# A hybrid encoder step: the recurrence's steps placed among the input projections, and the first unit's terms placed among the first transposes

## The chip, the cores and the metric

The kernel runs on one core of a Trainium2 chip. The metric is the device time of one execution in microseconds; all times below are microseconds from the first instruction of the profiled execution unless a unit is given.

## The reference

Two layers of an encoder run over 544 frames of 1024 features: 512 frames of a new stream and 32 frames of a running one, whose state is given. Only the mixer of layer 0 is touched.

```python
z = rmsnorm(x) @ w_in                    # (544, 3584): qa, ka, va | fb, ib, qb, gb, 512 each
qa, ka = rmsnorm per head of 64 with q_gain, k_gain
f = lb + (1 - lb) * sigmoid(fb);  logf = log(f);  kb = 1 - f;  qb = silu(qb);  vb = ib
# mixer A: softmax attention of 8 heads with a relative-position bias over (qa, ka, va)
# mixer B: S_t = diag(f_t) S_{t-1} + k_t v_t^T,  o_t = S_t^T q_t, in blocks
ob = rmsnorm per head(o) * out_gain * silu(gb)
x = x + concat(oa, ob) @ w_out
# then a mixture of 32 experts (2 for each frame); layer 1: short convolution, then experts
```

All inputs are float32. The outputs are the frames, the new keys and values, and the recurrence's and the convolution's new states.

## The kernel before

Every engine has an instruction list of its own, written out by hand; semaphores order them. Frames stand in five blocks `c` of 128, 128, 128, 128 and 32 (`ROWS`).

**Projections.** The 3584 columns of `w_in` are 14 groups of 256 (`HG`), in the order `GROUPS`: ib (groups 0, 1), fb (2, 3), qb (4, 5), gb (6, 7), qa (8, 9), ka (10, 11), va (12, 13). SyncE loads a group into one of three slots `wab` once the group three before it is done (`z_mm`, L355). ScalarE writes the rounded high part `wab_hi` (`group_hi`, L1075), GpSimd the rest `wab_lo` by one subtraction (L565). TensorE runs a group as units: five (one per block of frames) or, for groups 2 to 7, four (feature tile by half of the frames, transposed output). A unit is 24 matmuls: for each of 8 slices of the features, high by high, high by low and low by high (L661, L662). Unit `u` writes bank `u % 4` and waits until the unit four before it has been read out (`z_free`). There are 64 units, 0 to 63. Unit 0 alone runs its 8 terms with `wab_lo` last.

**The start.** Per block: ScalarE squares a block of frames (`square`), VectorE scales it to `XN` (`norm`, L1297), TensorE transposes it (`norm_transpose`, L637), ScalarE writes the high part `xc_hi`, VectorE the low part `xp_lo` (`mixer_in_lo`). TensorE transposes blocks 0 and 1, then unit 0, the transposes of block 2, unit 1, and so on.

**Read-out.** ScalarE turns groups 2 to 7 into `fT`, `qdecT`, `gateT`. Behind group 3, VectorE and ScalarE make `kinT` (keys with inverse decay) and `dec` from logarithm, scan and exponentials. For qa and ka, ScalarE squares a unit, VectorE sums (L1394, L1395), ScalarE takes the root, VectorE scales from the bank (L1398, which frees it) and multiplies by the gain.

**Recurrence.** For each block: transposes of `kinT` (`hgrn_keys`, L705) to `kr`; products of keys and queries (`hgrn_products`, L715), masked to `am`; state updates in groups of 32 frames (`hgrn_updates`, L731), chained by VectorE into states `st` (`hgrn_chain`, L1453, L1455); outputs (`hgrn_out`, L751 from `am`, L756 from `st`); ScalarE squares them, VectorE sums and scales them to `ot` (`hgrn_norm`, L1430); transposes of `ot` (`hgrn_T`, L767); VectorE multiplies by `gateT` into `zB` (`hgrn_gate`). Keys and products stand among the units of groups 12 and 13, together with the transposes of q and k (`rows_T`); updates, outputs and what follows stand behind the last unit, before the attention.

**Attention.** Scores (L806), VectorE adds the bias and takes the maximum (L1489), ScalarE the exponential (L1158), TensorE transposes (L823) and multiplies by the values (L839). `bias` is loaded from copies in device memory that SyncE writes early (L353) and reads behind the last unit (L367). Then follow the output projection (L880) and the experts, whose weights arrive in a stream.

## Time and profile before

| | |
|---|---|
| runs shown | 1215.63, 1217.22, 1218.97; median 1217.22 |
| profiled execution | 1213.17 |
| its span, first to last instruction | 1211.4 |
| TensorE matmul busy | 1019.1 (84%) |
| VectorE, ScalarE, GpSimd busy | 426.4, 289.8, 181.0 |
| mean granted TensorE clock | 0.92 |

The span is what the trace covers; the execution's own time is 1.8 longer. The granted clock is the share of full speed that the chip gave TensorE; its two levels are 1.2 GHz (0.50) and 2.4 GHz (1.00). A busy share is a mean over stages that have different limits, so it does not say what a stage waits for.

### The profile page before, as it was taken

To read this page: it belongs to the slowest core of one execution; us is meant where nothing else is said; L and a number is where in the kernel's file an instruction comes from. 1 tells how busy PE (TensorE), PEld (TensorE's weight loads), DVE (VectorE), ACT (ScalarE), POOL (GpSimd) and SP (SyncE) were. 2 spreads that over 40 slices of the span, in tenths; PEclk is the share of its full clock that TensorE was granted. 3 is DMA by queue.
4 is the path that set the end of the run, shared out by engine and by line. 5 is a ranking of instruction groups with operands and counts; after the bars stand their busy time and mean duration, and the time that the engine had idled before them with its cause. 6 is when DMAs were issued, how large, how long until landed. Compare 5 with 4: busy or idle time off the path is not lost.

```text
span 1211.4 us, 20104 instructions
## 1 busy us (share of the span) xinstructions
PE 1019.1 (84%) x8635; PEld 797.5 (66%) x8635; DVE 426.4 (35%) x907; ACT 289.8 (24%) x551; POOL 181.0 (15%) x146
## 2 busy tenths in 40 slices
PE   4998999777999899878778289999998999778771
PEld 4988999644689765444444089999997554444440
DVE  5324475356733611111101474555436111011104
ACT  4144332114721312111101332122212211111110
POOL 4334332002000023222111000000000122221110
PEclk9999999855989999999889689999999999888896
DMA  6322221411074599999997923324566999999966
GB/s 216 83 79 70 81 98 48 96 28 53 1 262 165 232 362 417 416 416 416 416 416 302 279 45 101 105 60 150 209 106 265 364 417 416 417 416 417 414 254 231
DMA packets 114862, 282.83 MB, mean 233 GB/s; under 512 B 22954, under 2 KB 70102, under 8 KB 98356
## 3 DMA queue, kind: packets, MB, share of 16 engines
q1 hardware_dynamic: 105044, 263.66, 58.5%
q0 software_dynamic: 9728, 17.85, 4.0%
q8 instruction: 70, 1.15, 0.4%
q14 instruction: 20, 0.16, 0.0%
HBM read 270.57 MB, written 27.02 MB: 246 GB/s over the span
## 4 chain that ended last, share of the span: by engine, by line
PE 59%; DMA 24%; DVE 7%; SPq 4%; ACT 2%; issue 2%; POOL 1%; DVEq 0%; POOLq 0%; ACTq 0%
DMA w<-in_w_dram 19%; PE banks L1015 12%; PE banks L943 12%; PE banks L880 9%; PE banks L662 8%; PE banks L954 4%; PE banks L661 3%; SPq L389 3%; DMA wab<-in_w_in_ab_dram 2%; DMA yab<-y_rows 1%; PE banks L637 1%; POOL wab_lo L565 1%; PE banks L839 1%; PE banks L823 1%; PE banks L937 1%
## 5 line engine op out<-in xcount | busy, mean ns | idle before, releaser
L943 PE MATMUL banks<-w,xgT 128*64 128x256 f32 x2048 | 253.2, 406 | 74.9 <-DMA w<-in_w_dram 73.7
L943 PEld LDWEIGHTS banks<-w,xgT 128*64 128x64 f32 x2048 | 159.4, 147 | 177.3 <-DMA w<-in_w_dram 77.4
L1662 DVE TENSOR_TENSOR hh<-banks,sg 128x128 f32<-128x128 f32 x64 | 18.7, 292 | 409.1 <-ACT sg L1230 409.1
L577 POOL DMA_INDIRECT y_rows<-ys,yidx x64 | 63.7, 995 | 383.3 <-ACT ys L1238 381.9
L954 PE MATMUL banks<-w,hT 128*64 128x512 f32 x512 | 116.9, 598 | 0.0
L1015 PE MATMUL banks<-xc_hi,wc_hi 128*128 128x272 f32 x384 | 111.4, 290 | 2.1 <-DVE xc_lo L1309 2.1
L1015 PE MATMUL banks<-xc_hi,wc_lo 128*128 128x272 f32 x384 | 111.7, 291 | 0.0
L1015 PE MATMUL banks<-xc_lo,wc_hi 128*128 128x272 f32 x384 | 110.9, 289 | 0.0
L573 POOL DMA_INDIRECT xr<-x_rows,gidx x32 | 33.5, 1046 | 412.4 <-DVE yidx L1648 394.4
L662 PE MATMUL banks<-wab_hi,xc_hi 128*128 128x256 f32 (+1 forms) x320 | 91.1, 285 | 0.7 <-POOL wab_lo L565 0.7
L662 PE MATMUL banks<-wab_hi,xp_lo 128*128 128x256 f32 (+1 forms) x320 | 90.1, 282 | 0.0
L662 PE MATMUL banks<-wab_lo,xc_hi 128*128 128x256 f32 (+1 forms) x320 | 88.4, 280 | 0.0
L1230 ACT ACTIVATE sg<-banks 128x128 f32<-128x128 f32 x64 | 17.8, 278 | 295.1 <-PE banks L943 295.1
L565 POOL TENSOR_TENSOR wab_lo<-wab,wab_hi 128x2048 fp32r<-128x2048 f32 x14 | 67.3, 4816 | 121.7 <-ACT wab_hi L1075 121.7
L1015 PEld LDWEIGHTS banks<-xc_hi,wc_hi 128*128 128x128 f32 x384 | 72.9, 190 | 2.7 <-issue 2.5
L1015 PEld LDWEIGHTS banks<-xc_lo,wc_hi 128*128 128x128 f32 x384 | 72.9, 190 | 0.0
L1015 PEld LDWEIGHTS banks<-xc_hi,wc_lo 128*128 128x128 f32 x384 | 72.7, 189 | 0.0
L954 PEld LDWEIGHTS banks<-w,hT 128*64 128x64 f32 x512 | 34.0, 136 | 58.7 <-issue 54.8
L661 PE MATMUL banks<-xc_hi,wab_hi 128*128 128x272 f32 x192 | 57.0, 297 | 6.7 <-POOL wab_lo L565 6.7
L1238 ACT ACTIVATE ys<-banks 128x512 f32<-128x512 f32 x64 | 38.2, 597 | 97.9 <-PE banks L954 97.9
L661 PE MATMUL banks<-xc_hi,wab_lo 128*128 128x272 f32 x192 | 56.9, 296 | 0.0
L662 PEld LDWEIGHTS banks<-wab_hi,xc_hi 128*128 128x128 f32 (+1 forms) x320 | 55.6, 174 | 1.7 <-POOL wab_lo L565 1.0
(283 smaller groups left out, 1796.0 us busy)
## 6 DMA issues: line engine op xcount, KB each, us to landing
w<-in_w_dram SPq DMA_DIRECT2D x192, 1024.0 KB, 23.2
wab<-in_w_in_ab_dram SPq DMA_DIRECT2D x13, 1024.0 KB, 5.0
wc<-in_w_in_c_dram SPq DMA_DIRECT2D x24, 512.0 KB, 5.7
yab<-y_rows SPq DMA_DIRECT2D x16, 512.0 KB, 6.8
wo<-in_w_out_ab_dram SPq DMA_DIRECT2D x4, 1024.0 KB, 5.6
x_rows<-XF SPq DMA_DIRECT2D x8, 512.0 KB, 2.6
wo<-in_w_out_c_dram SPq DMA_DIRECT2D x4, 1024.0 KB, 5.7
H<-in_x_prompt_dram SPq DMA_DIRECT2D x4, 512.0 KB, 8.4
```

Source lines behind the costliest of these rows:

```text
L389: sp.dma_start(w13[s][:, part, :, :], w[l, bass.ds(e, 1)].rearrange("e (p k) f -> p (e k) f", p=P)).then_inc(done, 16)
L565: pool.tensor_tensor(wab_lo[n % 3][:], wab[n % 3][:], wab_hi[n % 3][:].bitcast(F32), ALU.subtract).then_inc(w_lo, 1)
L573: pool.indirect_dma_start(xr[i][:, :], None, x_dram[l][:, :], bass.IndirectOffsetOnAxis(ap=index.bitcast(U32), axis=0), bounds_check=T - 1 ...
L577: pool.indirect_dma_start(y_dram[l][:, :], bass.IndirectOffsetOnAxis(ap=index.bitcast(U32), axis=0), ys[i][:, :], None, bounds_check=4 * T ...
L661: return pe.matmul(out, w[:, k, cols], x[:, k, t], **flags)
L662: return pe.matmul(out, x[:, k, t], w[:, k, :], **flags)
L880: last = pe.matmul(bank[i % 4][0:ROWS[c], 0:OW], z(a, k)[:, c * P:c * P + ROWS[c]], w(b, k, s), start=k == 0 and j == 0, stop=k == KT - 1 ...
L943: last = pe.matmul(bank[hb][64 * f:64 * f + 64, 0:2 * P].rearrange("p (w j) -> p w j", w=2), xgT[i][:, k, 64 * ab:64 * ab + 64], w13[s][:, ...
L954: last = pe.matmul(bank[6 + ab][64 * n:64 * n + 64, :], hT[ab][:, 64 * f:64 * f + 64], w2s[s][:, f, n * 512:(n + 1) * 512], start=f == 0, ...
L1015: last = pe.matmul(bank[3 * half + a][:, 0:HALF], w[s][:, k, a, :], x[:, k, half * HALF:(half + 1) * HALF], start=k == 0 and j == 0, stop= ...
L1238: act.activation(ys[e % 4][:], bank[6 + ab][:, :], ACT.Copy).then_inc(ys_ok, 1)
L1662: dve.tensor_tensor(hh[ab][:], bank[3 + ab][:, P:2 * P], sg[ab][:], ALU.mult).then_inc(hh_ok, 1)
```

## The change

1. **Start.** The two halves of the first weights are waited for and rounded one by one, with `xc_hi` of block 0 between them. Unit 0's terms with `wab_hi` run behind the transposes of block 0, then the transposes of blocks 1 and 2, then its terms with `wab_lo`. ScalarE's rounding of group 1 moves ahead of the square of block 4.
2. **Weights.** Group 3's load is issued ahead of the bias copies. ScalarE rounds group `n + 3` before the logarithm and the exponentials. GpSimd's subtraction is four instructions.
3. **Recurrence.** Keys and products stand behind units 27 to 31, the first updates behind unit 32, outputs behind units 34, 37, 40, 43 and 46 with the transposes of the block before and the updates of the next, the last transposes behind unit 48. Units 26 to 48 use banks 0 and 1 only; banks 2 to 7 belong to the recurrence. Unit 49 waits for all states and all of `zB`. The memory of `st`, `am`, `kr`, `osq`, `zB`, `bias` and one output weight moves.
4. **q and k.** ScalarE squares each head with a sum of its own, copies the unit to `q_tok` or `k_tok` and thereby frees the bank; VectorE scales in place. The gain of q moves into the copy behind its transposes.
5. **SyncE.** The state is loaded behind group 9, the new states are stored behind group 13's load, `bias` is loaded behind unit 53, and the first output weight no longer waits for `zB`.

```diff
+SHARED = range(FIRST[6], FIRST[11])
+UNIT_BANK = [u % 2 if u in SHARED else u % 4 for u in range(UNIT_END[-1])]
...
 @block.sync
-            sp.wait_ge(rev_ok, 1)
-            sp.dma_start(revs_dram[:, :, 0:639], bc(rev[:, 0:639].unsqueeze(1), [NH, 32, 639])).then_inc(rb_dma, 16)
             for n in range(3, 14):
                 sp.wait_ge(z_mm, UNIT_END[n - 3])
                 group_load(n)
+                if n == 3:
+                    sp.wait_ge(rev_ok, 1)
+                    sp.dma_start(revs_dram[:, :, 0:639], bc(rev[:, 0:639].unsqueeze(1), [NH, 32, 639])).then_inc(rb_dma, 16)
+                if n == 9:
+                    sp.wait_ge(hg_ok, 2)
+                    sp.dma_start(st[NPR][:], state_hgrn[0, 0].rearrange("(a b) k v -> (b k) a v", b=2)).then_inc(st_in, 16)
+            sp.wait_ge(st_ok, 4)
+            sp.dma_start(nh_p[0, 0].rearrange("(a b) k v -> (b k) a v", b=2), st[NPR - 1][:]).then_inc(sh_out, 16)
...
-            sp.wait_ge(z_mm, UNIT_END[-1])
+            sp.wait_ge(z_mm, UNIT_END[11])
...
-            sp.wait_ge(zB_ok, NC)
 @block.gpsimd
-                pool.tensor_tensor(wab_lo[n % 3][:], wab[n % 3][:], wab_hi[n % 3][:].bitcast(F32), ALU.subtract).then_inc(w_lo, 1)
+                for k in range(0, KT, 2):
+                    last = pool.tensor_tensor(wab_lo[n % 3][:, k:k + 2, :], wab[n % 3][:, k:k + 2, :],
+                                              wab_hi[n % 3][:, k:k + 2, :].bitcast(F32), ALU.subtract)
+                last.then_inc(w_lo, 1)
 @block.tensor
                 if u_ >= 4:
-                    pe.wait_ge(z_free[u_ % 4], u_ // 4)
+                    pe.wait_ge(z_free[b], freed(u_, b) - 1)
+                if u_ == SHARED.stop:
+                    pe.wait_ge(st_ok, NC)
+                    pe.wait_ge(zB_ok, NC)
...
                 if u_ == 0:
+                    norm_transpose(0, 1)
+                    norm_transpose(0, 2)
                     pe.wait_ge(w_lo, 1)
...
             for n in range(1, 14):
                 pe.wait_ge(w_lo, n + 1)
                 for a in range(UNITS[n]):
                     unit(n, a)
+                    beside = FIRST[n] + a - SHARED.start
+                    if 1 <= beside <= NC:
+                        hgrn_keys(beside - 1)
+                        hgrn_products(beside - 1)
+                    if beside == 6:
+                        hgrn_updates(0)
+                    if 8 <= beside <= 20 and beside % 3 == 2:
+                        c = (beside - 8) // 3
+                        if c > 0:
+                            hgrn_T(c - 1)
+                        hgrn_out(c)
+                        if c + 1 < NC:
+                            hgrn_updates(c + 1)
+                    if beside == 22:
+                        hgrn_T(NC - 1)
                     if n >= 12:
                         rows_T(NC * (n - 12) + a)
-                        i = NC * (n - 12) + a
-                        (hgrn_products if i % 2 else hgrn_keys)(i // 2)
-            hgrn_updates(0)
-            for c in range(NC):
-                if c + 1 < NC:
-                    hgrn_updates(c + 1)
-                if c > 0:
-                    hgrn_T(c - 1)
-                hgrn_out(c)
 @block.scalar
             square(0, 0)
-            group_hi(0)
-            for c in range(1, NC):
+            first_hi(0)
+            mixer_in_hi(0, [0])
+            first_hi(1).then_inc(w_hi, 1)
+            square(0, 1)
+            for c in range(2, NC):
                 square(0, c)
                 mixer_in_hi(0, [c - 1])
+                if c == 3:
+                    group_hi(1)
...
+                for h in range(heads):
+                    last = act.activation(qsq[i % 2][0:n, h * HD:(h + 1) * HD], bank[b][0:n, h * HD:(h + 1) * HD], ACT.Square,
+                                          accum_out=hss[0:n, sl + h:sl + h + 1])
+                last.then_inc(qsq_ok, 1)
+                act.activation((q_tok if i < 2 * NC else k_tok)[0:n, c, lo:lo + HG], bank[b][0:n, 0:HG], ACT.Copy).then_inc(z_free[b], 1)
+                act.wait_ge(qsq_ok, i + 1)
+                act.activation(hms[0:n, sl:sl + heads], hss[0:n, sl:sl + heads], ACT.Sqrt, bias=epsc[0:n, 0:1], scale=1.0 / HD).then_inc(qrt_ok, 1)
+                if i // 3 < NC and i % 3 == 0:
+                    hgrn_square(i // 3)
+                if i // 3 < NC and i % 3 == 1:
+                    hgrn_root(i // 3)
 @block.vector
             for i in range(4 * NC):
...
+                if i % 3 == 0 and 0 < i // 3 < NC:
+                    hgrn_gate(i // 3 - 1)
+                dve.wait_ge(qrt_ok, i + 1)
+                dve.reciprocal(hrs[0:n, sl], hms[0:n, sl]).then_inc(qms_ok, 1)
+                dve.wait_ge(qms_ok, i + 1)
+                scaled = dve.tensor_tensor(d, d, bc(hrs[0:n, sl].unsqueeze(2), four), ALU.mult)
...
+                c, step = divmod(i, 3)
+                if c < NC and step == 0:
+                    if c + 1 < NC:
+                        hgrn_chain(c + 1, 0)
+                    hgrn_sums(c)
+                    if c + 1 < NC:
+                        hgrn_chain(c + 1, 1)
+                if c < NC and step == 1:
+                    hgrn_norm(c)
+                if c == NC - 1 and step == 2:
+                    hgrn_gate(c)
```

## Rows read from the trace of the kernel before

**Rows 1.** The chain that ended last, to 200: start, us, what

```profile
13.12 4.08 DVE XN L1297
...
37.45 5.71 PE banks L662 x46
...
43.16 17.04 DMA wab<-in_w_in_ab_dram
...
62.21 4.55 POOL wab_lo L565
...
66.81 13.87 PE banks L661 x96
...
103.90 5.00 POOL wab_lo L565
...
108.94 25.92 PE banks L661 x192
...
134.86 59.48 PE banks L662 x504
```

**Rows 2.** The timeline: first updates on TensorE, first softmax instruction on VectorE

```profile
230.23 0.91 PE L731 MATMUL banks<-vb,kr 32*64 32x64 f32 x64
...
279.18 0.29 DVE L1489 CUSTOM_DVE_ANT_0 sneg<-banks,bias 128x128 f32<-128x128 f32 x1
```

**Rows 3.** Stretches: us, busy time of PE, PEld, DVE, ACT, POOL, clock, DMA share, GB/s

```profile
220.00:230.00 10.00, 10.00 (x151) 9.31 (x151) 1.91 (x5) 1.73 (x4) 0.00 (x0) 1.00 0.01 2
...
240.00:250.00 10.00, 5.17 (x155) 3.74 (x154) 4.03 (x9) 0.90 (x2) 0.00 (x0) 0.50 0.40 132
...
290.00:300.00 10.00, 7.94 (x32) 3.75 (x32) 6.67 (x14) 3.63 (x13) 3.82 (x1) 0.50 0.00 0
```

**Rows 4.** The timeline, TensorE in unit 0

```profile
19.43 0.41 PE L662 MATMUL banks<-wab_hi,xc_hi 128*128 128x256 f32 x1
...
19.65 0.41 PE L662 MATMUL banks<-wab_hi,xp_lo 128*128 128x256 f32 x1
```

**Rows 5.** Groups by line, VectorE's XN: busy us, mean ns, idle before

```profile
L1297 DVE SCALAR_TENSOR_TENSOR XN<-H,rstd,gmix 128x1024 f32<-128x1024 f32 x5 | 9.2, 1842 | 0.8 <-DMA gmix<-in_norm_mix_dram 0.6
```

**Rows 6.** The timeline, TensorE in the recurrence's steps

```profile
202.51 0.60 PE L705 MATMUL banks<-ident,kinT 128*128 128x128 f32 x4
...
252.49 1.28 PE L731 MATMUL banks<-vb,kr 32*64 32x64 f32 x64
...
256.38 0.67 PE L751 MATMUL banks<-vb,am 32*32 32x64 f32 x16
...
256.98 0.47 PE L756 MATMUL banks<-st,qdecT 64*32 64x64 f32 x16
...
257.38 0.67 PE L751 MATMUL banks<-vb,am 32*32 32x64 f32 x16
```

**Rows 7.** The timeline, ScalarE: exponential with sum, read of the sum, next exponential

```profile
279.51 0.40 ACT L1158 ACTIVATE pr<-sneg,nmaxs 128x128 f32<-128x128 f32 x1 [0.70 <-DVE nmaxs L1489]
...
279.82 0.19 ACT L1158 ACTIVATION_READ_ACCUMULATOR pr<-sneg,nmaxs 128x1 f32 x1
...
279.91 0.39 ACT L1158 ACTIVATE pr<-sneg,nmaxs 128x128 f32<-128x128 f32 x1
```

**Rows 8.** Groups by line on ScalarE and VectorE: value copies, ot, chain steps

```profile
L1137 ACT ACTIVATE va<-banks 128x256 f32<-128x256 f32 (+1 forms) x10 | 3.8, 379 | 26.0 <-PE banks L662 26.0
...
L1430 DVE TENSOR_TENSOR ot<-banks,hrs 128x512 f32<-128x512 f32 (+1 forms) x5 | 3.4, 689 | 0.2
...
L1455 DVE TENSOR_TENSOR st<-tmpS,dec 128x256 f32<-128x256 f32 x16 | 6.8, 425 | 0.5
```

**Rows 9.** The timeline: VectorE beside GpSimd's subtractions

```profile
181.51 3.96 DVE L1395 TENSOR_SCALAR hms<-hss 128x4 f32<-128x4 f32 x1
...
290.48 4.42 DVE L1511 TENSOR_TENSOR dg<-ident,rinv 128x1024 f32<-128x1024 f32 x1
...
287.25 6.57 POOL L560 TENSOR_TENSOR wo_lo<-wo,wo_hi 128x2048 fp32r<-128x2048 f32 x1
```

More of the change, by code:

```diff
@@ L306, in freed @@
         def freed(unit, b):
-            return len([u for u in range(unit + 1) if u % 4 == b])
+            return len([u for u in range(unit + 1) if UNIT_BANK[u] == b])
         class Chain:
@@ L693, in rows_T @@
                     pe.wait_ge(qkT_ok, i - 1)
+                else:
+                    pe.wait_ge(zt_ok, NC)
                 for m in range(4):
@@ L701, in hgrn_keys @@
                     pe.wait_ge(hg_ok, 2)
-                else:
-                    pe.wait_ge(a_ok, c)
+                if c >= 2:
+                    pe.wait_ge(ko_ok, c - 1)
                 for m in range(4):
-                    last = pe.transpose(bank[4][0:ROWS[c], m * P:(m + 1) * P], kinT[:, m, c * P:c * P + ROWS[c]], ident[:])
+                    last = pe.transpose(bank[6 + c % 2][0:ROWS[c], m * P:(m + 1) * P], kinT[:, m, c * P:c * P + ROWS[c]], ident[:])
                 last.then_inc(ko_mm, 1)
             def hgrn_products(c):
-                pe.wait_ge(ko_ok, c + 1)
+                if c < 2:
+                    for b in range(2 + 2 * c, 4 + 2 * c):
+                        pe.wait_ge(z_free[b % 4], freed(SHARED.start - 1, b % 4))
+                else:
+                    pe.wait_ge(a_ok, c - 1)
                 for m in range(4):
@@ L714, in hgrn_products @@
                             head = slice(64 * par, 64 * par + 64)
-                            last = pe.matmul(bank[4 + par][PAIR * r:PAIR * r + PAIR, m * PAIR:(m + 1) * PAIR], kinT[head, m, t],
+                            last = pe.matmul(bank[2 + 2 * (c % 2) + par][PAIR * r:PAIR * r + PAIR, m * PAIR:(m + 1) * PAIR], kinT[head, m, t],
                                              qdecT[head, m, t], start=True, stop=True)
@@ L730, in hgrn_updates @@
                             cols = slice((2 * m + par) * HD, (2 * m + par + 1) * HD)
-                            last = pe.matmul(bank[r][64 * par:64 * par + 64, m * HD:(m + 1) * HD], kr[c][rows, cols],
+                            last = pe.matmul(bank[2 + r][64 * par:64 * par + 64, m * HD:(m + 1) * HD], kr[c][rows, cols],
                                              vb[rows, c, cols], start=True, stop=True, tile_position=(PAIR * r, 64 * par))
@@ L799, in scores @@
                     pe.wait_ge(s_ok, 2 * j)
+                else:
+                    pe.wait_ge(qkT_ok, 2 * NC)
+                    for b in range(4):
+                        pe.wait_ge(z_free[b], freed(UNIT_END[-1] - 1, b))
                 if c == 4:
@@ L1112, in _ @@
                     act.wait_ge(z_mm, un + 1)
-                    act.activation(dst[:, m, half * HALF:(half + 1) * HALF], bank[un % 4][:, 0:HALF], fn).then_inc(z_free[un % 4], 1)
+                    act.activation(dst[:, m, half * HALF:(half + 1) * HALF], bank[UNIT_BANK[un]][:, 0:HALF], fn).then_inc(z_free[UNIT_BANK[un]], 1)
+                    if 1 <= un - SHARED.start <= NC:
+                        hgrn_key_rows(un - SHARED.start - 1)
             for i in range(4 * NC):
@@ L1437, in hgrn_gate, with hgrn_chain @@
                 dve.wait_ge(zt_mm, c + 1)
-                dve.tensor_tensor(zB[:, :, t], bank[4 + c % 2].rearrange("p (m t) -> p m t", m=4)[:, :, 0:n],
+                dve.tensor_tensor(zB[:, :, t], bank[2].rearrange("p (m t) -> p m t", m=4)[:, :, 0:n],
                                   gateT[:, :, t], ALU.mult).then_inc(zB_ok, 1)
-            def hgrn_chain(c):
+            def hgrn_chain(c, half):
+                groups = range(ROWS[c] // PAIR)[2 * half:2 * half + 2]
                 dve.wait_ge(u_mm, c + 1)
-                if c == 4:
+                if c == 4 and half == 0:
@@ new lines, in rows_T @@
+            def rows_T(i):
+                kind, c = divmod(i, NC)
+                src = bank[6 + i % 2][:, :].rearrange("p (m t) -> p m t", m=4)[:, :, 0:ROWS[c]]
+                dst = kT[:, :, c * P:c * P + ROWS[c]] if kind else qT[:, c, :, 0:ROWS[c]]
+                dve.wait_ge(qkT_mm, i + 1)
+                if kind:
+                    dve.tensor_copy(dst, src).then_inc(qkT_ok, 1)
+                else:
+                    dve.tensor_scalar(dst, src, qgain[:, 0:1], None, ALU.mult).then_inc(qkT_ok, 1)
```

238 lines of the change are left out of this document (113 added, 125 removed).

## Prediction

> **What bounds the kernel now.** I read the slices of the page first: TensorE is busy nearly everywhere until 420 us, then the expert weights' transfers set the pace. The change touches only the first layer's mixer, so the question is what that stretch loses today. The chain of waits, in order of time, answers it for the projections [rows 1]: TensorE is the chain except where it waits for a split of the weights. Three such places stand out. Group 3 starts at 66.81, groups 4 to 6 have two smaller waits, and the first frames wait for VectorE's `XN`. The timeline then shows the largest loss: the recurrence's first updates are issued at 230.23, when the projections are done, and VectorE's first softmax instruction of the attention comes at 279.18 [rows 2]. The stretches [rows 3] show what these 49 us are: TensorE half idle and its granted clock at 0.50 (1.2 GHz), after 1.00 (2.4 GHz) at 220 us where it was busy without a gap. The clock is still 0.50 at 290 to 300, inside the attention.
>
> **Units of price.** 504 matmuls of 256 columns take 59.48 [rows 1], so 0.118 each and 2.83 a unit (24 matmuls); at 272 columns I scale to 0.1254, 3.01 a unit, 12.04 a group of four. At 1.2 GHz the same matmuls start 0.22 apart [rows 4], 5.2 a unit.
>
> **The start, and first unit's terms among the transposes.** `XN` of frame block 1 took 4.08, where five took 9.2 in all, so 1.3 for each other one [rows 1, 5]. GpSimd's subtraction of the first weights, one instruction, ran beside it; it now comes in four. VectorE can wait for a piece, a quarter of 4.6, so 1.3 to 2.5: saved 1.6 to 2.8. The 16 terms of unit 0 that need no `wab_lo` come ahead of the transposes of blocks 1 and 2 and leave the path behind `XN`: 1.9 at 2.4 GHz, 3.5 at 1.2, I take 2.6. Against it: ScalarE now rounds both halves of the weights and copies `xc_hi` before the square of block 1, about 1 later, and the transposes of block 2 wait for that block's `XN`, which also comes one step later. I take 3.0 (0 to 4.4). Group 1 then no longer waits for `wab_lo`, since its rounding moves ahead of the last square; that is 0.8 more, estimated from the start at 37.45. **+3.8**.
>
> **Other orders of the weights.** Groups 1 and 2 are 14.2 and 12.0 of matmuls behind 37.45, so TensorE is ready at 63.65 and waits until 66.81: 3.2. The cause is group 3's load, which landed 17.04 after its issue behind the bias copies in the same queue [rows 1]. It now goes first, and the copies, needed late, have the time. Group 3 takes 13.87 instead of 12.04, because the clock must come back: 1.8. From its end, 80.68, two groups need 24.1, but group 6 starts at 108.94: waits of 4.2, for splits that ScalarE starts only behind its exponentials. They now come ahead of these. Groups 6 and 7 take 25.92 instead of 24.1: 1.8. The hidden cost is that the recurrence's inputs (logarithm, sums, exponentials) start a rounding later, 1.9, but their group ends 7 us earlier; they are due two units into group 6. **+11.0**. The load of the HGRN state and both state stores move ahead of the bias loads on SP. Their waits are met before SP's next load is due, or only outputs are queued behind them. The first output weights lose the wait for `zB`; they arrive about as late behind the start of the attention as now. These at nothing; if SP were held, a weight load needs 5 us and has a whole group (14) as cover.
>
> **The 49 us.** The steps leave the end of the projections: 48.95 from 230.23 to 279.18 go, and 1.5 remain for the last transposes, their copy and the fill of `bias` (estimated from the sizes). **+47.5**.
>
> **What TensorE does in their place.** Transposes and products of the keys only move, at equal cost. Into groups 7 to 10 come [rows 6]: updates, 0.91 at 2.4 GHz against 1.28 at 1.2, four and a short one: 4.0. The transposes of `ot`, like those of `kinT` 0.60, four and a short one: 2.8. The outputs: one quarter of a block starts 1.00 behind the last one at 1.2 GHz, so 4.0 a block; full clock was never seen. Lower bound half of it, upper bound no less than 4.0. Updates gained a factor 0.71, and I take that: 2.8, and 2.6 for the short block, which has the same four hand-overs: 13.8 in all (9.9 to 19.7). Switches between kinds of matmul: 1.5. **-22.1**.
>
> **Do the steps hide?** In this stage projections have two banks, so ScalarE must free a bank within one unit, 2.83. Squares with sums at 128 columns start 0.40 apart, the read of the accumulator included [rows 7]. For 64 columns I take 0.35 (bounds 0.2, the read alone, and 0.40), four make 1.4; the copy is 0.38 [rows 8]; the bank is free 1.8 behind the unit and with the root (0.2, estimated) the work is 2.0 (at most 2.3). It fits. Rounding a group's weights (1.9) fills a gap once in five units and delays one bank by some tenths.
>
> The round of three units is 8.5 + 0.6 + 2.8 + 0.9 = 12.8. On VectorE: updates ready at 4.3, eight chain steps of 0.425 with 0.03 between (3.7), the sums as long as `ot` (0.7): 8.7. The next unit ends at 7.1, ScalarE is done at 9.1, root and `ot` at 10.3 [rows 8]. So 2.5 to spare before the next round needs `ot`.
>
> **One new wait.** Unit 49 waits for all of `zB`. The last gate stands on VectorE behind key unit 14, which waits for ScalarE: 2.0, then 1.4 for three small instructions and the gate, less 0.4 of transposes: TensorE is idle 3.0, with all of groups 11 to 13 and the attention queued behind it. A wait of 3.2 cost 1.8 in clock, so 1.8 here too. **-4.8**.
>
> **The attention's start.** At 290 to 300 TensorE was busy 7.94 at 0.50 [rows 3]; at full clock that is 4 less in ten, 8 in twenty at best. VectorE and ScalarE take over part of the pace. VectorE's `dg` took 4.42, 3.3 of it until GpSimd's subtraction of the output weights was through [rows 9]; this can recur. I take **+5** (0 to 8).
>
> **A rule against the change.** VectorE's 181.51 instruction of four columns took 3.96, and `dg` ended 1.1 behind GpSimd's [rows 9]. The Trainium skill (SBUF — State Buffer, Who interferes with whom) says that VectorE and GpSimd share a port pair which one holds for a whole instruction, and that a VectorE instruction with both inputs in SBUF contends with a GpSimd instruction that reads SBUF. By that rule, the trace agrees. The new scaling reads `q_tok` and sums from SBUF, where it read a bank; the reduce and the small `tensor_scalar` go. By it VectorE pays up to 4.6 in a round beside such a subtraction, which is rival 2 (gain 21); by the durations of VectorE's rows alone [rows 8] the steps hide and the sum stays 40.4.
>
> **Sum.** 3.8 + 11.0 + 47.5 - 22.1 - 4.8 + 5 = 40.4. The profiled execution was 1213.17 (span 1211.4); 40.4 less is 1172.8. The median of the runs shown is 1217.22, 4 above; from it, **1177**. What follows hangs on the attention's end, so the gain moves down whole.
>
> **Rivals.**
> 1. Cheaper steps (outputs at 2.0 a block, +3.9; attention +8; no clock loss at unit 49, +1.8): gain 50, 1167. Chance 0.20. For it: outputs are many tiny matmuls without waits. Against: each quarter ends with hand-overs.
> 2. VectorE or ScalarE falls behind TensorE in the rounds. GpSimd's four pieces, 4.6 together, each taking turns with VectorE, lengthen the path from 10.3 to 14.9: 2.1 over the round; with other small lags 3.0 and 1.8 of clock, four rounds, 19. Gain 21, 1196. Chance 0.25. Against it: GpSimd works in only one group of five units.
> 3. The other side: the clock. If ScalarE needs over 2.83 a unit, two banks make TensorE wait in every unit, and with the gaps the clock falls to 1.2 GHz as it did at 240. Units 34 to 48 then cost 15 x 2.4 = 36 and outputs 6 more, groups 6 and 7 19: the gain of 40 is -21, 1238. It needs a ScalarE unit a fifth above my bound. Chance 0.04.
> 4. Nothing gained: the later stages are held by transfers that do not move up. Their issues wait for this very stage, so 1217; chance 0.02.
>
> **How the numbers follow.** The forecast has 0.49 and its own range is 1170 to 1185. To leave out no more than 2 in 10 the range goes to 1162 below (rival 1 beyond its value) and 1196 above (rival 2). A measurement of this kernel tells about 0.3% from no change (3.7 us). Faster: 0.94; within: 0.02; slower: 0.04.
>
> **What the profile will show.** Right: group 3 and group 6 start without a wait; granted clock 1.00 through groups 6 to 10; `hgrn_out` at 2.8 a block; one idle stretch of 3 before unit 49; first softmax instruction near 244. Wrong: waits before each round on `zt_ok` or `st_ok` (rival 2), on a bank (rival 3), a gap without releaser, as when code or data come late, or a clock that falls in the attention's first blocks.

## The result and the profile after

The changed kernel takes 1168.29 us (median of 4 runs, 1166.07 to 1169.81) where the kernel before took 1216.77 beside it: ratio 0.9598, 95% interval 0.9577 to 0.9619. That is 48.5 us less; the forecast was 1177 (range 1162 to 1196), 40 less. On a second chip the same pair gave 1171.38 and 1210.73, ratio 0.9671 [0.9651, 0.9692], 39.4 less. So the sign and the range held, and how well the size held depends on the chip: the same two kernels differ by 48.5 us on one and by 39.4 on the other. The traces tell more of the size than the medians.

| profiled execution | before | after |
|---|---|---|
| own time / span, us | 1213.17 / 1211.4 | 1169.81 / 1168.1 |
| mean granted clock | 0.920 | 0.936 |
| first softmax instruction on VectorE, us | 279.18 | 244.59 |
| first matmul of the first output projection, us | 338.98 | 299.50 |

Behind that first matmul of the output projection follow 872.4 us in before and 868.6 after. In the runs below this stretch is 869.3 to 874.3 for kernels with the recurrence moved and 871.5 to 873.1 for four without. It differs by some 5 us between profiled executions, without an order by what was changed in the mixer, so the change is to be read at 299.50: **39.5 us earlier**, against 40.4 in the sum. A second profiled execution of the changed kernel has this matmul at 297.71, 41.3 earlier.

The chain that ended last, kernel after, to 230: start, us, what. It answers to [rows 1] and [rows 6].

```profile
18.59 4.07 PE banks L677 x32
...
30.21 17.06 PE banks L677 x144
47.27 54.35 PE banks L676 x432
...
122.99 0.84 PE banks L754 x53
...
129.88 0.38 PE banks L774 x16
...
130.53 0.38 PE banks L774 x16
...
132.47 1.39 issue
133.86 0.91 PE banks L754 x53
134.78 10.26 PE banks L677 x72
145.04 0.44 PE banks L788 x4
...
148.91 8.55 PE banks L677 x72
...
185.11 5.78 PE banks L677 x48
190.91 0.90 ACT qsq L1190 x8
...
193.70 19.98 PE banks L677 x144
```

What to see: from 18.59 to 190.91 the chain is TensorE's alone. Group 1 starts at 33.05 (30.21 and one unit), and from there TensorE runs up to the first transposes of the keys without a wait; the 18 units of 272 columns take 3.02 each. Updates (L754), outputs (L774, L779) and transposes of `ot` (L788) are in the chain without a releaser: VectorE and ScalarE are never late in a round. Two places lose time: 1.39 us at 132.47 for which the trace names no reason, with 10.26 for the next three units where 8.55 is usual, and the wait before unit 49, after which 144 matmuls, six units, take 19.98 where six units at 2.83 are 17.0.

The timeline, kernel after: the normalisations at the start, unit 49 with the releaser of its wait, the first softmax instruction, `dg`. It answers to [rows 2], [rows 5] and [rows 9].

```profile
13.10 2.08 DVE L1357 SCALAR_TENSOR_TENSOR XN<-H,rstd,gmix 128x1024 f32<-128x1024 f32 x1
...
15.29 2.11 DVE L1357 SCALAR_TENSOR_TENSOR XN<-H,rstd,gmix 128x1024 f32<-128x1024 f32 x1
...
193.70 0.55 PE L677 MATMUL banks<-wab_hi,xc_hi 128*128 128x256 f32 x1 [1.70 <-DVE zB L1468]
...
244.59 0.29 DVE L1557 CUSTOM_DVE_ANT_0 sneg<-banks,bias 128x128 f32<-128x128 f32 x1 [0.16 <-PE banks L837]
...
254.82 1.79 DVE L1579 TENSOR_TENSOR dg<-ident,rinv 128x1024 f32<-128x1024 f32 x1
```

The stretches, kernel after: us, busy time of PE, PEld, DVE, ACT, POOL, clock, DMA share, GB/s. They answer to [rows 3].

```profile
130.00:140.00 10.00, 8.61 (x223) 7.74 (x215) 4.69 (x11) 3.82 (x19) 4.69 (x4) 0.83 0.16 55
...
190.00:200.00 10.00, 7.60 (x42) 7.22 (x41) 2.65 (x8) 3.95 (x19) 4.98 (x4) 0.66 0.56 172
...
250.00:260.00 10.00, 8.92 (x46) 4.46 (x47) 7.61 (x20) 4.72 (x17) 6.52 (x2) 0.61 0.27 97
```

Between 20 and 290 us the granted clock is below 1.00 in these stretches and in 240 to 250 (0.88) only: behind the two gaps and at the attention's start. The half clock of the 49 us [rows 3] is gone with the stretch.

One line of the 49 us in the kernel before, from the chain that ended last, was not read in the prediction:

```profile
238.67 4.60 issue
```

In the middle of the first block's outputs TensorE stands still for 4.60 us, and the trace names nothing that it waited for. So not all of the 49 us was a row of steps waiting for each other at half clock. In the kernel after, 1.39 us of the same kind are left, at 132.47.

ScalarE's squares with sums at 64 columns, kernel after, timeline; they answer to [rows 7]. They start 0.20 apart, the read of the sum included.

```profile
130.13 0.22 ACT L1190 ACTIVATE qsq<-banks 128x64 f32<-128x64 f32 x1
...
130.33 0.22 ACT L1190 ACTIVATE qsq<-banks 128x64 f32<-128x64 f32 x1
```

### The profile page after: what moved, and what is told of

Read it like the earlier page. It is cut to its first block, busy times and chain, and to the rows that moved or that the text cites. A ratio compares the mean times of both kernels' runs of the same rounds, so it can differ in the third digit from the quotient of the medians.

```text
span 1168.1 us, 20266 instructions
## 1 busy us (share of the span) xinstructions
PE 1013.1 (87%) x8635; PEld 793.4 (68%) x8635; DVE 389.6 (33%) x857; ACT 307.1 (26%) x712; POOL 189.8 (16%) x188
## 4 chain that ended last, share of the span: by engine, by line
PE 64%; DMA 19%; SPq 9%; DVE 5%; issue 2%; ACT 1%; POOL 1%; DVEq 0%; POOLq 0%; ACTq 0%
DMA w<-in_w_dram 15%; PE banks L1044 13%; PE banks L972 10%; PE banks L677 10%; PE banks L909 9%; PE banks L676 6%; SPq L396 6%; PE banks L983 5%; SPq L399 2%; PE banks L648 1%; PE banks L966 1%; DMA yab<-y_rows 1%; PE banks L870 1%; PE banks L854 1%; PE banks L837 1%
## 5 line engine op out<-in xcount | busy, mean ns | idle before, releaser
L972 PE MATMUL banks<-w,xgT 128*64 128x256 f32 x2048 | 261.6, 416 | 65.5 <-DMA w<-in_w_dram 64.3
L972 PEld LDWEIGHTS banks<-w,xgT 128*64 128x64 f32 x2048 | 162.2, 150 | 172.4 <-DMA w<-in_w_dram 72.7
L574 POOL TENSOR_TENSOR wab_lo<-wab,wab_hi 128x512 fp32r<-128x512 f32 x56 | 77.0, 1406 | 131.4 <-ACT wab_hi L1104 130.5
L677 PE MATMUL banks<-wab_hi,xc_hi 128*128 128x256 f32 (+1 forms) x320 | 94.4, 295 | 3.8 <-DVE xp_lo L1369 2.1
L677 PE MATMUL banks<-wab_hi,xp_lo 128*128 128x256 f32 (+1 forms) x320 | 93.0, 291 | 0.0
L677 PEld LDWEIGHTS banks<-wab_hi,xc_hi 128*128 128x128 f32 (+1 forms) x320 | 58.3, 182 | 5.1 <-issue 4.2
L677 PEld LDWEIGHTS banks<-wab_hi,xp_lo 128*128 128x128 f32 (+1 forms) x320 | 58.3, 182 | 0.4
L677 PEld LDWEIGHTS banks<-wab_lo,xc_hi 128*128 128x128 f32 (+1 forms) x320 | 56.9, 179 | 0.7 <-POOL wab_lo L574 0.3
```

Source lines behind the costliest of these rows:

```text
L574: last = pool.tensor_tensor(wab_lo[n % 3][:, k:k + 2, :], wab[n % 3][:, k:k + 2, :], wab_hi[n % 3][:, k:k + 2, :].bitcast(F32), ALU.subtract)
L677: return pe.matmul(out, x[:, k, t], w[:, k, :], **flags)
L972: last = pe.matmul(bank[hb][64 * f:64 * f + 64, 0:2 * P].rearrange("p (w j) -> p w j", w=2), xgT[i][:, k, 64 * ab:64 * ab + 64], w13[s][:, ...
```

## The experiments

Twelve kernels ran, four to a chip; each ratio is against the kernel before on the same chip (1210.73, 1213.02 and 1212.63 us). "Parts" below means GpSimd's subtraction of the low weights in four instructions instead of one. The changed kernel itself had the ratio 0.9598 on the first chip and 0.9671 on the second, so a difference of less than that (9 us) between ratios from two chips shows nothing by itself; there the traces decide.

### The changed kernel again, and the parts of its first half

The first is the changed kernel itself. The second has only the orders of the weights, on the kernel before:

```diff
-            sp.wait_ge(rev_ok, 1)
-            sp.dma_start(revs_dram[:, :, 0:639], ...)
             for n in range(3, 14):
                 sp.wait_ge(z_mm, UNIT_END[n - 3])
                 group_load(n)
+                if n == 3:
+                    ...
             group_hi(2)
+            group_hi(3)
...
             for n in range(6):
+                if n > 0:
+                    group_hi(n + 3)
...
-                group_hi(n + 3)
```

The third has only the start: unit 0's terms among the transposes, the first weights rounded by halves, group 1's rounding ahead of the last square, and the parts:

```diff
-                pool.tensor_tensor(wab_lo[n % 3][:], wab[n % 3][:], wab_hi[n % 3][:].bitcast(F32), ALU.subtract).then_inc(w_lo, 1)
+                for k in range(0, KT, 2):
+                    last = pool.tensor_tensor(wab_lo[n % 3][:, k:k + 2, :], ...)
+                last.then_inc(w_lo, 1)
...
+                    norm_transpose(0, 1)
+                    norm_transpose(0, 2)
                     pe.wait_ge(w_lo, 1)
```

The fourth has both, so that only the recurrence's move is missing. Expected:

> The changed kernel, unchanged, as the base for the others. The forecast's sum was 40.4 and the medians gave 48.5. Theory A (the sum of the prices of the mixer's stretch is right, and 4 to 9 more come from the later stages by chance of one execution or of one chip): 41 to 46 faster here. Theory B (the change itself makes the later stages faster): 48 or more again, and in the trace the time from the output projection's first matmul to the end is 4 or more shorter than in the kernel before.

> The kernel before with the other orders of the weights alone: group 3's load ahead of the bias copies, ScalarE's rounding ahead of the logarithm and exponentials. My sum: the two waits (3.2, 4.2) and two clock losses (1.8, 1.8) go: 11 faster, and the recurrence's 49 stay as they are. Rival: the waits before the groups only cover a wait that comes anyway (the recurrence's inputs are due later in this kernel, so none should): 5 or less.

> The kernel before with the start alone: first unit's terms among the transposes, first weights rounded in halves, GpSimd's subtractions in four pieces. My sum 3.8, measured in the changed kernel's trace 4.4 up to group 1. But group 3's load stays where it is behind the bias copies, and these wait for VectorE's small copies. If the load's landing does not move up with group 1, the 4.4 turns into a longer wait before group 3 and 0 to 2 is left; if it moves up, 4.

> The kernel before with start and orders together, so all of the change but the recurrence's move (and the squares on ScalarE). By my sum 14.8 faster, 15.2 by the trace of the changed kernel; the recurrence's move is then worth the rest, 47.5 - 22.1 - 4.8 + 5 = 25.6 by my sum, 33 if the medians' 48.5 hold. The rival, that the early groups gain nothing for a recurrence that still stands behind the last unit, gives 0 to 5.

Measured: the changed kernel 1171.38, ratio 0.9671; orders alone 1207.2, 0.9962 [0.9945, 0.9978]; start with parts 1201.5, 0.9919 [0.9900, 0.9938]; both 1194.9, 0.9865 [0.9843, 0.9886]. The changed kernel gained 39.4, less than either theory had; in its trace 869.3 us follow the output projection's first matmul, 3.1 less than in before. The recurrence's move is what is left between the last two kernels, 1194.9 and 1171.38: 23.5 us, against 25.6 in the sum. Start and orders together are as expected (15.8 us), the split is not: the orders gave a third of their 11.0, the start with the parts 9.2 instead of 3.8. The chain with orders alone says why:

```profile
79.69 5.60 DVE kinT L1363
...
92.24 4.46 DVE dec L1370
...
104.43 25.90 PE banks L662 x192
130.33 59.48 PE banks L663 x504
```

The groups' splits now come earlier, and so GpSimd's one long subtraction (4.60 at 67.28, 4.76 at 79.36, 4.82 at 91.79) lies on VectorE's short ones: `kinT` takes 5.60 and a copy of 68 columns 4.46. ScalarE's exponentials wait for these, the bank that group 6 needs is read out behind the exponentials, and group 6 starts at 104.43, where 16 units of 3.02 from 52.90 would end at 101.2. So the orders remove the wait before group 3, and a wait before group 6 stays.

### The parts alone, and the changed kernel without them

The first is the kernel before with the four instructions of the diff above and nothing else. The second is the changed kernel with one instruction again:

```diff
-                for k in range(0, KT, 2):
-                    last = pool.tensor_tensor(wab_lo[n % 3][:, k:k + 2, :], ...)
-                last.then_inc(w_lo, 1)
+                pool.tensor_tensor(wab_lo[n % 3][:], wab[n % 3][:], ...).then_inc(w_lo, 1)
```

> The kernel before with one edit: GpSimd's subtraction for the low part of a group's weights in four pieces instead of one. The prediction gave the pieces nothing of their own; by the two runs with parts of the change, the start's edits with the pieces brought 9.2 us and the orders without them 3.5. Theory A (the one-piece subtraction holds VectorE up and this is what the waits of groups 3 to 6 come from): the decay and the keys on VectorE take about 1.5 and 1.3 us again instead of 4.46 and 5.60, the wait before group 6 goes, and the kernel is 5 to 6 us faster than before (about 1205 where before is 1211). Theory B (the pieces only help once the first block starts earlier or the orders are changed): within 0.3%, group 6 still late.

> The changed kernel with GpSimd's subtraction as one instruction again. In the run with the orders of the weights alone, VectorE's kinT took 5.60 instead of 1.3 behind such an instruction and group 6 began late. Theory A (one instruction of GpSimd holds VectorE for its whole length, four pieces only for one): XN of block 1 at 4.1 instead of 2.1, kinT at 5.6, ScalarE's exponentials 4 later, TensorE waits for a bank at group 6 and the clock falls: 6 to 8 slower than the changed kernel. Rival (the pieces change nothing but the start): 2 slower.

Measured: parts alone 1205.07, ratio 0.9933 [0.9909, 0.9958], 8 us faster (5 to 11 by the interval; 5 to 6 were expected); the changed kernel without them 1180.55, 0.9726 [0.9698, 0.9754], 6.7 us behind the changed kernel's 0.9671 by the ratios of two chips, and in the traces 10.7 and 12.5 behind its two executions at the output projection (310.23). The chain with the parts alone, then groups by line on VectorE between 60 and 130 for the changed kernel without the parts, then the same for the changed kernel:

```profile
51.25 24.17 PE banks L664 x192
...
78.05 1.31 DVE kinT L1363
...
83.28 7.37 POOL wab_lo L566 x4
...
90.69 38.03 PE banks L664 x288
128.72 59.47 PE banks L665 x504
```

```profile
L1418 DVE TENSOR_SCALAR kinT<-fT 128x2176 f32<-128x2176 f32 x1 | 5.6, 5586 | 0.0
...
L1425 DVE COPY dec<-cumT 128x68 f32<-128x68 f32 x1 | 4.4, 4446 | 0.0
```

```profile
L1421 DVE TENSOR_SCALAR kinT<-fT 128x2176 f32<-128x2176 f32 x1 | 2.3, 2274 | 0.0
```

The same instruction costs 1.3 us with GpSimd idle, 2.3 beside the parts and 5.6 beside the one subtraction. GpSimd pays for it: four parts take 5.0 to 7.4 where one instruction takes 4.5 to 5.1. That trade is right where VectorE's work is short and awaited. In the kernel before, four scans `cumT` took 9.19 in the chain; with the parts alone 6.9, and group 8 starts at 128.72 instead of 134.86 [rows 1]. The Trainium skill (SBUF — State Buffer, Who interferes with whom) has VectorE and GpSimd share a port pair that one of them holds for a whole instruction; these durations agree with it: with the orders alone `kinT` starts 0.33 behind a subtraction of 4.76 and ends 1.17 behind its end.

Most of the 6.1 us does not come from the scans, however. Groups 2 and 3 run through here (51.25, 24.17 for eight units), 5.3 earlier at their end than in the kernel before (75.42 against 80.68), and behind them one wait for a split is left, 3.2 before group 5. The wait before group 3 is gone although its load still stands behind the bias copies. The timeline says why, first before, then with the parts alone:

```profile
37.46 4.76 DVE L1332 COPY rev<-rel 8x384 f32<-8x384 f32 x1
```

```profile
36.84 1.43 DVE L1335 COPY rev<-rel 8x384 f32<-8x384 f32 x1
```

SyncE's bias copies wait for this short copy of VectorE, which lay beside GpSimd's subtraction; with it the load of group 3 is issued at 39.21 instead of 43.16 [rows 1].

The start of group 8 shows how the 15.1 us add up in this order; in another order the shares differ:

| kernel | group 8 starts | earlier by |
|---|---|---|
| before [rows 1] | 134.86 | |
| parts alone | 128.72 | 6.1 |
| start and parts | 124.94 | 3.8 more |
| start, parts and orders | 119.76 | 5.2 more |

The orders alone bring 4.5 (130.33), and the start without the parts brings nothing: in the changed kernel with the one subtraction `XN` takes 4.14 and 4.17 for two blocks, and group 1 starts at 38.7, later than the 37.45 of before. There group 8 starts 12.0 later than in the changed kernel (139.02 against 127.03, both with the keys' steps ahead of it). Either the orders or the parts remove the wait before group 3; the later one, before group 5 or 6, goes only with both.

The chain with start and parts, and with the orders as well:

```profile
59.37 12.34 PE banks L664 x96
...
86.98 37.95 PE banks L664 x288
124.94 59.48 PE banks L665 x504
```

```profile
47.29 72.47 PE banks L665 x576
119.76 59.48 PE banks L666 x504
```

### The outputs twice

The changed kernel with every output quarter of a block computed twice; the first copy is overwritten.

```diff
-                for m in range(4):
+                for m in [0, 1, 2, 3] * 2:
                     out = [bank[6 + par][:, m * HD:(m + 1) * HD] for par in range(2)]
```

> The changed kernel with every matmul of the recurrence's outputs issued twice (the second time over the same bank with the same result): 2.6 more a block on TensorE, 2.3 for the short one. Theory A (the steps stand on TensorE's path at full clock, as summed): 12.7 slower than the changed kernel. Rival (a part of the step's time is a wait for VectorE or ScalarE that the second set fills): 8 or less. More than 15 if instruction supply fails, as in the gap of 1.4 behind the first output.

Measured: 1191.23, ratio 0.9820 [0.9791, 0.9849], 18 us more than 0.9671; by the traces the output projection starts 20.4 and 22.2 later (319.87). Its chain:

```profile
132.68 1.40 issue
134.08 0.45 PE banks L774 x16
...
182.98 1.52 issue
...
186.98 10.73 PE banks L677 x72
```

The added products cost what they cost before, 0.65 a quarter, 12.7 in all; the rest are two more gaps without a releaser (0.80 and 1.52, beside the 1.40 that was there) and the clock behind them: three units take 10.73 instead of 8.55.

### More work for ScalarE in every unit

The changed kernel with twelve more squares with sums into unused space for each unit of 64-column heads, 2.4 us on top of 1.4.

```diff
+                for j in range(12):
+                    h = j % heads
+                    act.activation(junk[0:n, j * HD:(j + 1) * HD], bank[b][0:n, h * HD:(h + 1) * HD],
+                                   ACT.Square, accum_out=rsum[0:n, j:j + 1])
                 for h in range(heads):
                     last = act.activation(qsq
```

> The changed kernel with 12 more squares with sums a unit on ScalarE, at 0.20 each: 2.4 more, so a bank is free 3.7 behind its unit and ScalarE's work is 3.9 a unit. It tests the rival in which two banks make TensorE wait in each unit and the clock falls. By that rival units 34 to 48 run at 1.2 GHz: 15 x 2.4 + 6 = 42 slower or more. By the plain sum of waits, 10 units without steps behind them wait 0.9 each, some 9 slower, and at most 12 with what is lost at the round's start, if the clock stays.

Measured: 1183.24, ratio 0.9756 [0.9729, 0.9784], 10.3 us more than 0.9671; by the traces 12.1 and 13.9 more at the output projection (311.64). The plain sum of waits had 9 to 12. One of its stretches:

```profile
160.00:170.00 10.00, 7.97 (x218) 7.12 (x218) 6.10 (x13) 6.37 (x56) 3.68 (x4) 0.83 0.02 4
```

TensorE waits for banks (8.0 busy of ten here, 9.1 in 140 to 150 and in 170 to 180), and the clock dips to 0.83 here and is 1.00 in the other two. ScalarE at 3.5 to 3.7 us a unit, well above rival 3's 2.83, costs its waits and no collapse to half clock. One reason is in the chain: three units with the recurrence's steps between them last 12.4 on TensorE (145.04 to 157.47), not 8.5, so ScalarE has about 4.1 a unit.

### The last block earlier

The wait before unit 49 hangs on the last block's root, normalisation and gate. Here they come one unit earlier, and its transposes behind unit 47.

```diff
-                    if beside == 22:
+                    if beside == 21:
                         hgrn_T(NC - 1)
...
-                if i // 3 < NC and i % 3 == 1:
+                if i // 3 < NC and i % 3 == (0 if i // 3 == NC - 1 else 1):
                     hgrn_root(i // 3)
...
+                if i == 3 * NC - 2:
+                    hgrn_gate(NC - 1)
...
-                if c < NC and step == 1:
+                if c < NC and step == (0 if c == NC - 1 else 1):
                     hgrn_norm(c)
-                if c == NC - 1 and step == 2:
-                    hgrn_gate(c)
```

> The changed kernel with its last small steps earlier: for block 4 the root and the scaling to ot follow the sums at once, its transposes stand behind unit 47 instead of 48, its gate ahead of key unit 13. Theory A: the wait before unit 49 (2.4 idle in the trace of the changed kernel, and 6 units in 19.98 instead of 17.0 behind it because of the clock) goes: 5 faster than the changed kernel (0.4%). Rival: the wait is only passed on (to unit 49's bank or to GpSimd's split): 0 to 1.

Measured: 1167.73, ratio 0.9629 [0.9605, 0.9654], against 0.9671 and 0.9598 for the changed kernel on two other chips: the times don't show a gain. The chain does: TensorE goes through (188.39, 168 matmuls in 19.89), and the output projection starts at 294.90, where the changed kernel's two executions have 299.50 and 297.71. The second execution of the changed kernel adds a finding: the same wait, but behind it

```profile
193.82 17.25 PE banks L677 x144
```

that is 0.25 us lost in clock instead of 3.0, with a clock of 1.00 in 190 to 200. The same wait stands in five more of these kernels up to here: 17.24 with the idle products alone, 18.72 to 18.77 in three, 19.39 with the added squares, where the wait is longer. So it costs 0.2 to 3 us more in clock; nothing in the traces says why.

### The load of group 9 later

The gap near 132.5, at the tail of group 9's load, was in every run of the changed kernel with that load in its place (1.02 to 1.45; at 144.46 in the one without the parts, which is that much later). Here that load, and the rounding behind it, start after the second block's updates.

```diff
                 sp.wait_ge(z_mm, UNIT_END[n - 3])
+                if n == 9:
+                    sp.wait_ge(u_mm, 2)
                 group_load(n)
...
-                if i % NC == 0:
+                if i == 2 or (i > 0 and i % NC == 0):
                     group_hi(9 + i // NC)
```

> The changed kernel with the load of group 9's weights held back until the second block's updates are done, and its copy to the high part put behind two more of the recurrence's waits. Tested is the gap of 1.4 us in which TensorE waits for nothing that the trace shows, behind the first block's outputs near 132.5 us. Theory A (the load in flight delays TensorE's instructions): the gap goes, the clock of 0.83 in 130 to 140 us with it, 2 to 3 us faster than the changed kernel, ratio near 0.963 where that had 0.9655 to 0.967. Theory B (the gap belongs to the dense row of small products itself): still 1.3 to 1.5 us there, and no difference beyond 0.3%. If the load is then too late for group 9, a wait for it shows before its first unit and the kernel is slower.

Measured: 1168.06, ratio 0.9625 [0.9589, 0.9661]. The chain and the stretch:

```profile
132.05 0.38 PE banks L776 x16
132.70 0.84 PE banks L756 x53
133.54 8.75 PE banks L679 x72
```

```profile
130.00:140.00 10.00, 10.00 (x248) 9.17 (x248) 5.92 (x15) 5.97 (x24) 0.00 (x0) 1.00 0.56 169
```

The gap is gone, the clock is 1.00, and unit 48 ends at 188.17 instead of 190.91: 2.7 us. The kernel before and the four others whose recurrence stands behind the last unit have a gap of 4.5 to 4.7 at the same outputs (238.67 in before), with the bias loads in flight. In this run GpSimd's parts (140.86 to 146.22) lie beside the second block's outputs (142.7 to 145.3), without a gap, so they alone are not the cause; with the load away from the outputs the gap is gone. A load alone isn't enough either: the next-to-last block's outputs (170.45 to 173.04) lie beside one in the changed kernel without a gap, and only twice as many of them, beside the same load, had the 1.52 above. How a load delays instructions that wait for nothing wasn't tried; the changed kernel's profile lists a DMA queue for instructions (8 packets between 100 and 150), and that they queue behind the load is argued only. By the time alone the gain isn't certain, since the changed kernel's interval on another chip overlaps.

### Idle products at the attention's start

The first is the changed kernel with idle products on TensorE in four steps of the attention, the second has the last block earlier as well.

```diff
                 if t == 8:
                     cached_T()
+                if 1 <= t <= 4:
+                    idle_products(7, 4)
```

> The changed kernel with the idle products in the attention's first steps alone. Theory A: the granted clock in 250 to 260 us rises from 0.61 to 0.9 or more and the output projection starts 2 to 3 us sooner, ratio near 0.964. Theory B: the clock rises, the output projection starts no sooner, ratio 0.966 to 0.968. By both, the kernel with the two additions is 4 to 6 us faster than this one.

> Two additions to the changed kernel: the last block's root, normalisation and gate one step earlier with the transposes of its product behind unit 47 (5 us by the ratios of the earlier runs), and idle products on TensorE in the first steps of the attention, where the granted clock was 0.61 in 250 to 260 us. Theory A (the attention's start is bound by TensorE at the lower clock): 2 to 3 us on top, ratio 0.960 to 0.961. Theory B (it is bound by the softmax's chain over VectorE and ScalarE, so the clock there costs nothing, and the idle products only lie in the way): as the first addition alone, 0.963, or up to 0.965.

Measured: 1169.02, ratio 0.9639 [0.9602, 0.9677]; and **1164.45, 0.9596 [0.9560, 0.9633]**, the fastest kernel of this study by its median. Against the kernel with only the last block earlier (0.9629) the intervals overlap. The chain with idle products alone, and with both:

```profile
255.07 4.43 DVE dg L1581
```

```profile
247.29 2.16 DVE dg L1581
...
291.17 13.86 PE banks L911 x97
```

The stretch 250 to 260 of the kernel with both, and of the one with idle products alone:

```profile
250.00:260.00 10.00, 10.00 (x78) 5.36 (x74) 8.18 (x27) 7.65 (x26) 3.84 (x1) 1.00 0.01 2
```

```profile
250.00:260.00 10.00, 5.38 (x39) 3.38 (x39) 9.97 (x12) 1.77 (x9) 8.33 (x2) 0.82 0.00 1
```

With both, the clock holds at 1.00 and the output projection starts 3.7 us before that of the kernel with the last block earlier alone (294.90). It was 1.7 ahead already before the attention (168 matmuls behind the switch start at 186.66, not 188.39), so 2.0 fall in the attention: the lower end of theory A, from one execution of each. `dg` is not the reason, since it takes 1.87 there and 2.16 here. Alone, the idle products fell in an execution (its slowest of six, 1178.38 where four lie between 1168.2 and 1169.6) in which TensorE has a gap of 1.80 without a releaser at 252.16 and `dg` takes 4.43 beside GpSimd's subtraction of the output weights, as it did before [rows 9]; the output projection starts at 303.01. This one execution says nothing on the clock's worth, and no other was profiled.

## Why the prediction was right

| step | predicted | measured at |
|---|---|---|
| start | +3.8 | +4.4 (37.45 to 33.05); 3.8 by group 8's table |
| orders of weights | +11.0 | +10.7 behind that, but 6.1 of the 15.1 in the table are the parts |
| the 49 us | +47.5 | +47.9 (48.95 less the 1.0 from the last transposes to the first softmax instruction) |
| added TensorE steps | -22.1 | -18.8 by length, -1.2 for slower units beside the keys, -3.1 for the gap and its clock |
| wait before unit 49 | -4.8 | -2.4 wait, -3.0 clock (second execution -0.25) |
| attention's start | +5 | +4.9 (279.18 to 338.98 is 59.8; 244.59 to 299.50 is 54.9) |
| whole, at the output projection | 40.4 | 39.5 |

**What bounds the kernel** was right: in the kernel after, TensorE is the chain up to the output projection but for the wait before unit 49 and short pieces of the attention, and what the sum takes off and adds on TensorE is what the time does. The 49 us went but for 1.0; the first softmax instruction came at 244.59, forecast near 244. What they were was read in part only: 4.60 of them are the gap at 238.67, which the prediction put down to steps in a row and the clock. It went with the rest, so the sum didn't suffer.

**The start.** VectorE's `XN` took 2.08 and 2.11, in the middle of 1.3 to 2.5. Right in size, but only with the parts: without them the start alone would have put group 1 later than before (38.7), since `XN` of a second block then takes 4.17 too. And the split into four instructions was counted only here, for the wait of one `XN`.

**The orders.** This is the step that failed, though its sum came out by luck: the prediction put the waits down to group 3's load standing behind the bias copies, and to splits that ScalarE starts only behind its exponentials. That is half of the truth, and the sum came out only because the parts, counted for `XN`, did the rest. The orders without the parts gave 4.5 at group 8 and 3.5 in time, and the parts without the orders 6.1. The bias copies were late because VectorE's copy `rev` took 4.76 beside GpSimd's subtraction, and the exponentials because the scans lay beside another (`cumT` 9.2 for four, in the trace of before); with the orders alone `kinT` and `dec` lay there instead. The prediction had read such an instruction at 181.51 and beside `dg` [rows 9], and didn't look for it on this chain.

**The added steps.** Updates took 0.84 to 0.91 (4.0 in all, as predicted), transposes 0.44 (2.2, not 2.8), outputs 0.65 a quarter, so 2.6 a block and 2.3 for the short one, with 12.7 against 13.8. Twice the outputs cost their length again: the price is that of small products, not of hand-overs. The switches between kinds, 1.5 in the sum, show as six units from 102.74 on at 3.20 to 3.23 instead of 3.02, 1.2 in all. So 2.1 were saved against the sum, and 3.1 went into what it hadn't: the gap of 1.39 and 1.7 of clock behind it. That the two nearly cancel is luck. The prediction named such a gap as a sign of being wrong; it was there, and small.

**Do the steps hide.** Yes. ScalarE's squares came at 0.20, the lower bound, and a unit is done in about 1.4, not 2.0. Rival 2 (19 us) didn't come: no round waits for VectorE. Its mechanism is real in another form: with the one-piece subtraction in the changed kernel 12.0 us are lost by the start of group 8's units, all ahead of the rounds (5.7 at the start with `XN`, the rest with `kinT` and `dec`), and in the rounds one `q_tok` takes 3.44, with a short wait of TensorE behind it. So it is the parts that keep it away. Rival 3 named a threshold at 2.83 for ScalarE and a clock at half; 3.5 to 3.7 cost 10 to 14 us, and the clock stayed at 0.83 or above through the rounds. Its price of 61 was wrong by a factor of four to six.

**The wait before unit 49** was the right wait, 0.6 shorter than predicted. Its clock is 0.2 to 3 and not a constant 1.8, and with the wait taken away the output projection starts 4.6 and 2.8 earlier than in the two executions, where the sum had 4.8 for both.

**The attention's start** was right in size, and for mixed reasons. `dg` took 1.79 instead of 4.42, so the wait for GpSimd did not recur: that is up to 2.6 of the 4.9. The clock was not full, as the prediction's upper bound had it: it fell again in the first blocks, to 0.88 and 0.61, which the prediction had named as a sign of being wrong.

**Rival 1** has the measured median of the first chip (1167 against 1168.3), but not for its reasons: outputs at 2.6 and not 2.0, attention 4.9 and not 8. Of the 9 us between the trace's 39.5 and the medians' 48.5, 3.8 lie behind the output projection, where executions differ by 5 anyway; the profiled execution of before was 3.6 under its median of 1216.77, and that of after 1.5 above its own, and where in the kernel those 5.1 lie no trace shows. On the second chip the difference is 39.4. What makes the kernel before slower on one chip than on another (1216.8 against 1210.7) stays open.

## What to carry to other kernels

A row of dependent small steps that runs by itself costs its length and TensorE's clock. Laid between independent matmuls it costs only its own TensorE time, and that sum can be made beforehand from the trace; check that the engine that frees the banks needs less than one unit. Cut GpSimd's long elementwise instructions where VectorE has short ones that others wait for: it was one loop, worth 8 us in the kernel before and 7 to 12 in the changed one. And when two edits aim at the same waits, run each alone before saying which did it: here the sum was right and the split was not. A gap without a releaser in the trace of before is worth a question of its own: here 4.6 of the 49 us were one.

## What the runs showed of the hardware that was not expected

- One VectorE instruction of 2176 columns took 1.3, 2.3 or 5.6 us, and a copy of 68 columns 0.23, 1.1 or 4.45, with GpSimd idle, in four short instructions, or in one long one. A copy of 384 columns on 8 partitions took 4.76 beside the long one and 1.43 beside the four; the DMA that waited for it, and the load behind that in the queue, were issued 4 us later.
- Dense small matmuls (128 in 2.6 us) had a gap of 1.0 to 1.45 us without a releaser behind them when a load of 1 MB had been in flight beside the first of them, and none when the load came later; with the bias loads, four of 512 KB, in flight the gap was 4.5 to 4.7. A load beside a later block of them left no gap.
- The same 2.4 us of waiting cost 3.0 us of clock in one execution and 0.25 in another. With the added squares, stretches with TensorE busy 8 to 9 of ten kept a granted clock of 0.83 to 1.00; in the kernel before a stretch at 7.94 of ten had 0.50 (290 to 300), and in the kernel after one at 8.92 had 0.61 (250 to 260). So the busy share of ten us does not tell the clock.
